# Unread identity products in TensorE's gaps, gates evicted later with one sigmoid per branch, head norms by rows

## The reference, cut to what matters

```python
# RWKV branch, 8 heads of 64
kk = heads(k * k_k)
kk = kk * lax.rsqrt(jnp.maximum(jnp.sum(kk * kk, -1, keepdims=True), 1e-24))
...
y = wkv7_scan(rh, heads(decay), kh, vh, -kk, kk * ah)
mean = jnp.mean(y, -1, keepdims=True)
var = jnp.mean(jnp.square(y - mean), -1, keepdims=True)
y = ((y - mean) * lax.rsqrt(var + RWKV_GN_EPS)).reshape(Bsz, L, D_RWKV)
...
# second block's mixer
gates = jax.nn.sigmoid(proj[..., OFF_GATE:] + gate_b).reshape(Bsz, L, N_BRANCHES, D_MODEL)
merged = (gates[..., 0, :] * (y_a @ w_up_rwkv)
          + gates[..., 1, :] * (y_b @ w_up_moba)
          + gates[..., 2, :] * (y_c @ w_up_ssm))
return merged @ w_out
```

## Time and profile before

| | us |
|---|---|
| median of 3 runs (lowest, highest) | 1753.09 (1752.62, 1755.78) |
| the profiled execution | 1758.4 |
| its span in the trace | 1757.2 |
| TensorE busy | 1525.5, 87% |
| TensorE weight loads (beside products) | 1277.4, 73% |
| VectorE busy | 1010.5, 58% |
| ScalarE busy | 785.3, 45% |
| GpSimd busy | 228.9, 13% |
| mean granted TensorE clock | 0.916 |

### The profile page before, as it was taken

One profiled execution on the slowest core, in us unless ns is written; L12 is line 12 of the kernel. 1 busy time (PEld: TensorE's weight loads), 2 busy tenths in 40 slices (PEclk: granted clock), 3 DMA queues, 4 the chain that ended last, 5 costly groups with the idle time before them and its releaser, 6 DMA issues. The chain is left out here.

```text
span 1757.2 us, 21641 instructions
## 1 busy us (share of the span) xinstructions
PE 1525.5 (87%) x8851; PEld 1277.4 (73%) x8851; DVE 1010.5 (58%) x1254; ACT 785.3 (45%) x1142; POOL 228.9 (13%) x337
## 2 busy tenths in 40 slices
PE   2988879997988879998978879989958589999996
PEld 1977769896877769997877777767947466666664
DVE  6567456666565344445474536583344656666665
ACT  3455255445465354444543213423100376666662
POOL 5321100001141000002880002120001000000000
PEclk9899889999898889999999997989959699999998
DMA  9756168776471055654432130202203369999982
GB/s 346 248 200 204 43 213 286 263 269 204 153 274 39 4 189 191 192 192 134 144 116 77 49 108 25 72 25 73 97 0 110 157 245 339 349 342 349 338 312 94
DMA packets 134585, 310.32 MB, mean 177 GB/s; under 512 B 6239, under 2 KB 99766, under 8 KB 114902
## 3 DMA queue, kind: packets, MB, share of 16 engines
q1 hardware_dynamic: 130326, 299.18, 48.7%
q0 software_dynamic: 3584, 8.71, 1.9%
q10 hardware_dynamic: 576, 1.05, 0.2%
HBM read 307.87 MB, written 1.05 MB: 176 GB/s over the span
## 5 line engine op out<-in xcount | busy, mean ns | idle before, releaser
L312 DVE TENSOR_TENSOR mlp_weights_lo<-weights,mlp_weights_hi 128x2048 fp32r<-128x2048 f32 x64 | 146.5, 2291 | 68.1 <-ACT mlp_weights_hi L302 67.1
L3510 DVE TENSOR_TENSOR expert_pair_lo<-weights,expert_pair_hi 128x2048 fp32r<-128x2048 f32 x53 | 119.9, 2290 | 64.3 <-ACT expert_pair_hi L3501 64.3
L253 PE MATMUL bank<-mlp_in_hi,mlp_weights_hi 128*128 128x256 f32 x512 | 147.3, 288 | 10.3 <-DVE mlp_in_lo L696 10.3
L254 PE MATMUL bank<-mlp_in_lo,mlp_weights_hi 128*128 128x256 f32 x512 | 146.9, 287 | 0.0
L255 PE MATMUL bank<-mlp_in_hi,mlp_weights_lo 128*128 128x256 f32 x512 | 146.8, 287 | 0.0
L302 ACT ACTIVATE mlp_weights_hi<-weights 128x2048 fp32r<-128x2048 f32 x64 | 121.9, 1908 | 55.6 <-issue 46.3
L253 PE MATMUL bank<-expert_pair_hi,x_block_hi 128*128 128x512 f32 x280 | 114.0, 407 | 5.3 <-issue 5.3
L255 PE MATMUL bank<-expert_pair_hi,x_block_lo 128*128 128x512 f32 x280 | 110.4, 394 | 0.0
L254 PE MATMUL bank<-expert_pair_lo,x_block_hi 128*128 128x512 f32 x280 | 110.2, 394 | 0.0
L253 PEld LDWEIGHTS bank<-mlp_in_hi,mlp_weights_hi 128*128 128x128 f32 x512 | 100.3, 196 | 12.1 <-issue 11.1
L564 DVE SCALAR_TENSOR_TENSOR ada<-weights,cond,ada 128x2048 f32<-128x2048 f32 x42 | 100.1, 2384 | 2.1 <-DMA weights<-in_w_ada 1.5
(11 more groups left out here) (739 smaller groups left out, 3849.2 us busy)
## 6 DMA issues: line engine op xcount, KB each, us to landing
weights<-in_w_ada SPq DMA_DIRECT2D x48, 1024.0 KB, 5.3
weights<-in_w_in SPq DMA_DIRECT2D x45, 1024.0 KB, 5.4
weights<-in_expert_w_gate SPq DMA_DIRECT2D x35, 1024.0 KB, 5.3
weights<-in_w_up SPq DMA_DIRECT2D x32, 1024.0 KB, 5.5
weights<-in_w_down SPq DMA_DIRECT2D x32, 1024.0 KB, 5.2
weights<-in_expert_w_up SPq DMA_DIRECT2D x18, 1024.0 KB, 6.8
weights<-in_expert_w_down SPq DMA_DIRECT2D x18, 1024.0 KB, 7.3
expert_raw<-in_expert_w_up SPq DMA_DIRECT2D x17, 1024.0 KB, 6.3
```

Source lines behind the costliest of these rows:

```text
L253: pe.e.matmul(out, lhsT[0], rhs[0], start=start, stop=False)
L254: pe.e.matmul(out, lhsT[0], rhs[1], start=False, stop=False)
L312: dve.e.tensor_tensor(lo, ring.view(name), hi.bitcast(F32), SUB).then_inc(*dve.mark(*self.key, "low", n))
L3510: dve.e.tensor_tensor(pair[1][:, :, part], expert_raw(s, kind, n), pair[0][:, :, part].bitcast(F32), SUB).then_inc(*dve.mark("expert", "lo ...
```

## The change

Three edits. First, `keep_going` issues products of the identity with itself into the first 128 columns of a bank that is free at that point. Nobody reads them. It stands at 13 places, 248 products in all. At the start of layer 1 a wait for the modulation ("mod", 1, 0) is put ahead of them.

Second, the gates of RWKV and S5 are evicted without the sigmoid (Identity with bias), one turn later, and each branch gets one sigmoid over its whole 128x2048 tile: S5's behind its eighth part, RWKV's at the end of the gates. VectorE waits for "gates done". S5's gates are made first, in a tile of their own (`s5_gates`, printed `s_gates`), and RWKV's later, in `rw_bk`, once the scan has read it.

Third, the head norms of `kk` and `var`: eight products give one total for each token and head (tokens on the partitions, 128x16), the maximum (or scale and shift), square root and reciprocal run on 128x16, and 16 products with the identity spread the 16 columns back over the 64 rows of each head, into two banks; VectorE multiplies straight from PSUM.

The diff, cut: the waits and banks of `head_spread_tensor` and the changes of names that follow from these are left out.

```diff
+def keep_going(c, pe, bank, count):
+
+    for _ in range(count):
+        pe.e.matmul(bank[:, 0:P], c.identity, c.identity, start=True, stop=True)
...
     for t in range(TT):
         yield from turned_rows_tensor(c.rows.pe, c.row_banks, c.work, t, ("mixer norm", 0, "rows"), "mixer in", 0)
+    keep_going(c, c.rows.pe, c.banks[4], 26)
     yield from some_steps(ada, KT)
+    keep_going(c, c.rows.pe, c.banks[4], 23)
     for l, s in enumerate(c.layers):
         if l:
+            yield from c.rows.pe.wait_ge("mod", l, 0)
+            keep_going(c, c.rows.pe, c.banks[7], 13)
             for t in range(TT):
                 yield from turned_rows_tensor(c.rows.pe, c.turn_banks, c.work, t, ("mixer norm", l, "rows"), "mixer in", l)
+            keep_going(c, c.rows.pe, c.banks[7], 20)
...
         yield from out_rows_tensor(c, c.out, ("out", l), s.hT, s.out_pieces, turned[0])
+        keep_going(c, c.out.pe, c.banks[4], 18)
         yield from turned[1]
+        keep_going(c, c.out.pe, c.banks[4], 15)
         yield from meet(c, "tensor", l, "out")
...
         yield from turned_rows_tensor(c.rows.pe, c.turn_banks, c.x, t, ("mlp out norm", DEPTH - 1, "x"), "x cols")
+    keep_going(c, c.rows.pe, c.banks[7], 18)
...
 def gates_scalar(c, s, act, banks, branch, gates, spaces=0):
+
+    kind = ACT.Identity if spaces else ACT.Sigmoid
     for n in range(4):
         yield STEP
+        if spaces:
+            yield STEP
         yield from act.wait_ge("gates", branch, n)
...
-            ins = act.e.activation(gates[:, 2 * n + j, :], src[:, j, :], ACT.Sigmoid, bias=s.v["gate_b_2"][:, f:f + 1])
+            ins = act.e.activation(gates[:, 2 * n + j, :], src[:, j, :], kind, bias=s.v["gate_b_2"][:, f:f + 1])
         ins.then_inc(*act.mark("read", "gates", branch, n))
-        for _ in range(1 + spaces):
-            yield STEP
+        yield STEP
+    if not spaces:
+        act.also("gates done", branch)
+
+
+def gates_end_scalar(act, branch, gates):
+    yield from act.wait_ge("read", "gates", branch, 3)
+    act.e.activation(gates, gates, ACT.Sigmoid).then_inc(*act.mark("gates done", branch))
...
+def head_totals_tensor(c, pe, banks, src, *key):
+
+    yield from pe.wait_ge(*key, "squares")
+    bank = yield from banks.take(pe, *key, "totals")
+    for t in range(TT):
+        for k in range(4):
+            n = HEADS * t + 2 * k
+            ins = pe.e.matmul(bank[:, n:n + 2], src[:, k, t * P:(t + 1) * P], c.head_sum[:, 0:P:64], start=True, stop=True)
+    ins.then_inc(*pe.mark(*key, "totals"))
+
+
+def head_spread_tensor(c, pe, banks, rows, *key):
...
+                    ins = pe.e.matmul(bank[64 * e:64 * e + 64, at:at + P], rows[:, n:n + 1].to_broadcast([P, 64]), c.identity,
+                                      start=True, stop=True)
+        ins.then_inc(*pe.mark(*key, "spread", k0))
...
-    yield from head_sums_tensor(c, pe, banks, s.rw_work, "rw kk")
+    yield from head_totals_tensor(c, pe, banks, s.rw_work, "rw kk")
     yield STEP
     yield from lora_tensor(c, s, 3)
     yield STEP
+    yield from head_spread_tensor(c, pe, banks, s.heads, "rw kk")
     yield STEP
...
-    yield STEP
     yield from dve.wait_ge("rw kk", "root")
-    dve.e.reciprocal(s.ka, s.ka).then_inc(*dve.mark())
-    dve.wait_own()
-    dve.e.tensor_tensor(s.kk, s.kk, s.ka, MULT).then_inc(*dve.mark())
-    dve.wait_own()
+    dve.e.reciprocal(s.heads, s.heads).then_inc(*dve.mark("rw kk", "inverse"))
+    yield STEP
+    for k in range(0, 4, 2):
+        yield from dve.wait_ge("rw kk", "spread", k)
+        dve.e.tensor_tensor(s.kk[:, k:k + 2, :], s.kk[:, k:k + 2, :], as_cols(banks.of("rw kk", "spread", k)), MULT).then_inc(
+            *dve.mark("read", "rw kk", "spread", k))
...
-AHEAD = (1, 13, 0), (0, 14, 1), (2, 4, 1)
+AHEAD = (1, 13, 0), (2, 14, 1), (0, 4, 1)
...
+    keep_going(c, pe, c.banks[7], 22)
     yield from pe.wait_ge("pairs")
...
+    keep_going(c, pe, c.banks[7], 34)
     yield from pe.wait_ge("slots")
...
         ins.then_inc(*pe.mark("slot T", b0))
+    keep_going(c, pe, c.banks[7], 15)
...
     c.ring.closed = True
+    keep_going(c, pe, c.banks[4], 11)
     yield from turned[1]
```

More of the change, by code:

```diff
@@ L2147, in add_branch_vector @@
             yield from dve.wait_ge("branch up", branch, half, k)
-            yield from dve.wait_ge("read", "gates", branch, f // 2)
+            yield from dve.wait_ge("gates done", branch)
             src = as_cols(banks.of("branch up", branch, half, k))
@@ L2165, in rwkv_memory @@
 def rwkv_memory(s, mem):
-    s.rwkv_gates = mem.new("rwkv_gates", 8, SEQ)
+    s.s5_gates = mem.new("s5_gates", 8, SEQ)
     s.gates_at = mem.at - 8 * SEQ
@@ L2171, in rwkv_memory @@
     bk = mem.new("rw_bk", 8, SEQ)
-    s.b, s.k, s.s5_gates = bk[:, 0:4, :], bk[:, 4:8, :], bk
+    s.b, s.k, s.late_gates = bk[:, 0:4, :], bk[:, 4:8, :], bk
     s.bend, s.kend = mem.new("rw_bend", 4, SEQ), mem.new("rw_kend", 4, SEQ)
     s.bk_at = mem.at - 16 * SEQ
+    s.heads = mem.new("rw_heads", 2 * HEADS)
     s.chunk_decay, s.v_cols = mem.new("rw_chunk_decay", 4, N_CHUNK), mem.new("rw_v_cols", 4, SEQ)
@@ L2186 @@
 flat4 = lambda v: v.rearrange("p k s -> p (k s)")
+def head_totals_tensor(c, pe, banks, src, *key):
[7 more added lines that the diff above has]
+def head_spread_tensor(c, pe, banks, rows, *key):
+    yield from pe.wait_ge(*key, "inverse")
+    for k0 in range(0, 4, 2):
+        bank = yield from banks.take(pe, *key, "spread", k0)
+        for k in range(k0, k0 + 2):
+            for t in range(TT):
+                at = (k - k0) * SEQ + t * P
+                for e in range(2):
+                    n = HEADS * t + 2 * k + e
+                    ins = pe.e.matmul(bank[64 * e:64 * e + 64, at:at + P], rows[:, n:n + 1].to_broadcast([P, 64]), c.identity,
+                                      start=True, stop=True)
+        ins.then_inc(*pe.mark(*key, "spread", k0))
 def head_sums_tensor(c, pe, banks, src, *key):
@@ L2275, in rwkv_input_vector @@
     yield STEP
[L2276 to L2279, removed]
+    yield from dve.wait_ge("rw kk", "totals")
+    dve.e.tensor_scalar(s.heads, banks.of("rw kk", "totals")[:, 0:2 * HEADS], 1e-24, None, MAX).then_inc(
+        *dve.mark("read", "rw kk", "totals"))
     dve.also("rw kk", "sums")
@@ L2631, in rwkv_output_tensor @@
     yield STEP
-    yield from head_sums_tensor(c, pe, banks, flat_work(s), "rw var")
+    yield from head_totals_tensor(c, pe, banks, flat_work(s), "rw var")
     yield STEP
+    yield from head_spread_tensor(c, pe, banks, s.heads, "rw var")
     yield STEP
@@ L2642, in rwkv_output_scalar @@
 def rwkv_output_scalar(c, s):
-    act, work = c.rw.act, flat_work(s)
+    act = c.rw.act
     yield STEP
@@ L2646, in rwkv_output_scalar @@
     yield from act.wait_ge("rw var", "sums")
-    act.e.activation(work, work, ACT.Sqrt).then_inc(*act.mark("rw var", "root"))
+    act.e.activation(s.heads, s.heads, ACT.Sqrt).then_inc(*act.mark("rw var", "root"))
     yield STEP
@@ L2662, in rwkv_output_vector @@
     dve.e.tensor_tensor(work, yT, yT, MULT).then_inc(*dve.mark("rw var", "squares"))
-    for k in range(0, 4, 2):
-        yield from dve.wait_ge("rw var", k)
-        dve.e.tensor_scalar(work[:, k:k + 2, :], as_cols(banks.of("rw var", k)), 1.0 / 64, 64e-5, MULT, ADD).then_inc(
-            *dve.mark("read", "rw var", k))
-    dve.also("rw var", "sums")
-    yield STEP
-    yield from dve.wait_ge("rw var", "root")
-    dve.e.reciprocal(work, work).then_inc(*dve.mark())
-    dve.wait_own()
-    dve.e.tensor_tensor(yT, yT, work, MULT).then_inc(*dve.mark())
+    yield from dve.wait_ge("rw var", "totals")
+    dve.e.tensor_scalar(s.heads, banks.of("rw var", "totals")[:, 0:2 * HEADS], 1.0 / 64, 64e-5, MULT, ADD).then_inc(
+        *dve.mark("read", "rw var", "totals"))
+    dve.also("rw var", "sums")
+    yield from dve.wait_ge("rw var", "root")
+    dve.e.reciprocal(s.heads, s.heads).then_inc(*dve.mark("rw var", "inverse"))
+    yield STEP
+    for k in range(0, 4, 2):
+        yield from dve.wait_ge("rw var", "spread", k)
+        dve.e.tensor_tensor(yT[:, k:k + 2, :], yT[:, k:k + 2, :], as_cols(banks.of("rw var", "spread", k)), MULT).then_inc(
+            *dve.mark("read", "rw var", "spread", k))
     dve.wait_own()
@@ L2681, in rwkv_output_vector @@
     yield STEP
-    yield from add_branch_vector(c, s, dve, banks, 0, 2, s.rwkv_gates, s.bend[:, 0:2, :])
+    yield from add_branch_vector(c, s, dve, banks, 0, 2, s.late_gates, s.bend[:, 0:2, :])
 def moba_memory(s, mem):
@@ L3094, in side_branches_scalar @@
     yield from s5_scalar(c, s)
+    yield from gates_end_scalar(act, 2, s.s5_gates)
     for half in range(2):
@@ L3122, in gates_ahead_scalar @@
 def gates_ahead_scalar(c, s):
-    for (branch, steps, spaces), gates in zip(AHEAD, (s.merged, s.rwkv_gates, s.s5_gates)):
+    for (branch, steps, spaces), gates in zip(AHEAD, (s.merged, s.s5_gates, s.late_gates)):
         for _ in range(steps):
             yield STEP
-        if branch == 2:
+        if branch == 0:
```

(1 more changed line is left out.)

4 lines of the change are left out of this document (2 added, 2 removed).

## The result

The changed kernel takes 1725.97 us (four runs, 1721.19 to 1727.2) against 1752.87 (four runs): ratio 0.9824, 95% interval 0.9806 to 0.9842. The ratio isn't the quotient of these two medians, which is 0.9847 and lies just outside the interval: by the medians the saving is 27 us, by the ratio 31. Measured again later, in another set, it takes 1720.44 us (five runs) against 1758.1 (17 runs): 0.9781, 0.9763 to 0.9800, which is 38 us. The four runs of the kernel before in the first comparison lie at 1752.6 to 1755.8; in the later sets most of its runs gather near 1753 or near 1758 (some reach 1766), and its profiled execution (1758.4) is one of the latter. The profiled executions are 33 us apart (1758.4 and 1725.5).

A forecast was written before the change was run, and what follows sets the result against it. TensorE's products, their granted clock and its idle places bound the kernel. Identity products 18.1, gates 7.4 and 0, kk 6.5 and var 3.8 sum to 35.8 us off a 1753.1 median: 1717 us, range 1702 to 1736.

The forecast's parts named there:

- What bounds the kernel, and what a gap costs: TensorE's products and clock set the end; a gap costs its length plus about 2.3 us of half-speed work.
- All fit at 0.22 and then end before what TensorE waits for: Identity products in the hand-over, join and tail gaps: at 0.22 us each, their own cost is nothing.
- rival A: Identity products run at 0.44 us each and outlast their gaps, overruns 22.5 us in sum: 1764 us; chance 0.05.
- The term of 7.5: Tail: the clock kept by identity products speeds transposes, router and first expert products, saving 7.5 us (1 to 9).
- L3233 at 3.5 us: Tail: the router's 16 products would take 3.5 us instead of 7.01.
- 7.4 and 0: Gates: 7.4 us saved in the S5 stretch (4.4 shorter waits, 3.0 clock), 0 (-2 to +2) at the gates' end.
- 3 us in sum or less: S5 stretch: TensorE's waits there would sum to 3 us or less.
- 6.5 forecast: kk head norm: the short reciprocal removes TensorE's 6.14 us wait, less the spread products' cost; saves 6.5 us (5 to 8).
- 3.8 forecast: var head norm: new chain of 5.0 to 8.9 us replaces 10.9; gain 2.5 to 6.4, taken as 3.8.
- B: S5 stretch: the eviction's new place puts ScalarE's angle chain in front, S5 gains nothing: 1726 us; chance 0.12.
- C: Identity products fit but don't hold the clock, so part 1 gives nothing: 1735 us; chance 0.13.
- D: S5 stretch keeps full clock throughout (9.5 for 3.0), var's small products run fast (2.6 more): 1708 us; chance 0.10.

The follow-up runs named there:

- the filled kernel at 1715: Changed kernel with gaps filled almost to their ends, plus 56 more identity products in gaps of the second block: 1715.38 us, 0.9749 of the kernel before.

## Why the prediction came out as it did

The time lay in the range (1702 to 1736) and missed the likeliest case's own range (1710 to 1724) by 2 us in the first comparison; it met it when measured again. The sum of 35.8 us was near the 27 to 38 measured, and that nearness is in part luck: taken alone, the tail and kk gave 5.3 us less than forecast, the gates and var 5.8 more, and the middle lost time that the forecast put at nothing. By steps:

**What bounds the kernel, and what a gap costs.** Right in kind. Where the clock was kept, the work behind the gaps ran at 1.00 and the hand-overs gave 3.1 us each against 3.2. The price of 0.22 a product was 0.23 at most places; it was 0.29 at the join, where the granted clock is 0.51 in the first 2 us, and 0.27 for the first 26 at the start, at a clock of 1.00, which isn't explained. All places ahead of the tail gave 12.1 in the trace against 10.6. By medians all 13 places gave 13.7 alone and some 19 beside the other parts, against a forecast of 18.1.

**The tail.** The step "All fit at 0.22 and then end before what TensorE waits for", with the full clock taken to stay behind them, failed for the profiled execution: 11 products left 1.67 us idle, the clock fell, and 22 at the lower level outlasted the gap, which is rival A in a small place. The term of 7.5 measured 5.0 by medians, and the sign "L3233 at 3.5 us" didn't come: 7.01. The failed assumption is that the gap partly filled would do there: filled, the same router product took 3.73. At the hand-overs it did do, with as much left idle (1.70 and 1.82 us), so what is left idle doesn't decide alone; what else does isn't shown.

**Gates.** The size was low (7.4 and 0 against 10.7) and the reason given was wrong. The forecast said that ScalarE's time was idle anyway and that the sines' place ahead of the eviction is what counts. Without the loads' removal that place gave nothing (0.9998), and the removal of the 11 loads at the old place gave 8.2. At the end of the gates I had weighed 2.1 gained against as much lost; the trace of the gates alone shows 4.8 gained by 1235 (the wait 3.7 to 1.5, and the low clock behind it gone) and 2.0 given back behind it, where the wait for bank 7 (1.7) stands. The sign "3 us in sum or less" for the S5 stretch came only in part: 1.6 and 0.6, but 2.5 more at its end. The Trainium skill's figure in "ScalarE: Activation LUTs", section "What ACT_TABLE_LOAD costs", of 1380 ns of drain beside the load still shows in no row here: the 34 loads left are 1.28 us each, as before, all but the first start 0.02 us behind ScalarE's work before them, and in 19 cases the next activation starts 0.01 us behind the load. That 11 loads are worth 8.2 us, 0.75 each, is less than the load itself; that the rest lay in ScalarE's idle time is likely but not shown.

**kk.** Right in its place, mis-sized in the end: 6.5 forecast, 4.6 to 6.2 gained by 900 in the traces, 3.7 by the ratio. Then 2.2 to 5.9 us go back between 940 and 1040, in every one of the eight traces that arrive there 5.7 us or more earlier than the kernel before and have no products in these gaps. The forecast counted the clock only at the gaps that it filled, not at those that shift. That it is the shift and not the norms' own doing is supported by three things: the identity products alone lose 3.9 there too, the four traces that shift this work by 2.4 us or less (among them the gates alone) lose nothing, and with those gaps filled nothing is lost. So it isn't the chance of one execution. Why the same gap costs the clock in one alignment and not in another isn't shown.

**var.** 3.8 forecast, 6.3 measured alone (3.7 to 9.1), 5.7 in the trace. The new chain ran from 1266.65 to the end of the spread at 1273.58, 6.9 us, in the middle of the forecast's 5.0 to 8.9, and to the multiply's end at 1274.32; the forecast had taken it nearer to the slow end. The up projection added 1.2 us, 15.68 instead of 16.84, which the forecast hadn't counted. The sign of "about 10 instead of 13.65" is the 9.2 us with the spread inside; idle were 5.5.

**The base.** The sum was carried from an execution of 1758.4 to a median of 1753.1 as if it were the same program 0.3% faster. But the median of before is itself 1753 in one set and 1757 to 1758 in the others, and the forecast was set against the lowest. Against its own set the saving was 27 us in the first comparison (31 by the ratio) and 38 in the other, and 33 between the two profiled executions that the sum was made for, so the sum is off by 3 there. Why the sets differ isn't settled.

**Rivals.** B (the angle chain bounds S5) didn't happen: the S5 stretch gained 6.5 to 8.9 in the traces with the gates' edit whole. Its mechanism is there in small: ScalarE's waits for GpSimd's angle in that stretch grew from 6.9 to 10.7 us, but VectorE's waits for the sines fell from 23.6 to 18.1. C (no clock held) is refuted by the windows. D (1708) wasn't reached, though the filled kernel at 1715 comes near by holding the clock elsewhere. A happened at one of 13 places (22 products outlasted their gap).

## What to carry to other kernels

Where an engine's clock falls behind a gap, the gap's price is its length plus the slow work behind it; filling it with products nobody reads can return the second part. How much idle time may be left isn't one number here: 1.7 us left did no harm at the hand-overs and cost the clock in the tail, 0.34 did no harm in either. A count sized for the full clock can outlast the gap when it starts at the low one. Count function-table loads that stand between an engine's release and the next one's bank before moving the instructions around them: the move alone was worth nothing here. When a saving shifts later work, look for it again at the end of the next section with small gaps, and judge by many runs: two traces of the same changed kernel differ by 3.6 us in one stretch.

## What the runs showed that was not expected

Waits of the same length (2.15, 3.43 and 2.69 us) stood at a clock of 1.00 in the kernel before (956 to 1007) and at 0.77 to 0.84 in the same work 6 to 3 us earlier. In the tail idle pieces of 1.67 and 0.78 us were followed by 0.50; at the hand-over two of 1.70 and 1.82 us were followed by no loss. ScalarE's square root on 128x16 takes 0.22 us and VectorE's reciprocal 0.25, against 6.55 for the reciprocal on 128x1024: a 64th of the elements for a 26th of the time.
